# Two heads' value products in alternate column halves, score and turn in one step, and a new placing of the gate pieces in a two-layer hybrid trunk

## The chip, the cores and the metric

The kernel runs on one core of a Trainium2 chip. The metric is the device time of one execution in microseconds, median of the runs shown. Everything is computed in one launch: two layers, 512 latent and 128 context tokens (640 columns together), width 1024.

## The reference

Each layer has a mixer with four branches, a gated merge, an output projection and an MLP. What matters here is the two attention branches and the merge:

```python
# branch A: latent attention, 4 heads, value width 64
s = einsum('bqhd,bkhd->bhqk', q, k) * scale
p = softmax(s);  o_a = einsum('bhqk,bkhd->bqhd', p, v)
# branch D: differential attention, 4 heads, two score maps per head, value width 64
p = softmax(s1) - lam * softmax(s2);  o_d = einsum('bhqk,bkhd->bqhd', p, v)
o_d = rmsnorm(o_d, da_norm_w) * (1 - lam_init)
# merge: four branches, eight blocks of 128 output columns each
proj  = einsum('blnc,ncd->blnd', [o_a, o_b, o_c, o_d], w_branch)
gates = sigmoid(h @ w_gate)
mix   = sum_n(gates * proj) @ w_out
x     = x + gt_a * mix
```

Latent queries see all 640 keys, context queries only the 128 context keys. All data is fp32; the dense products with `h` and with the merged sum are made of three fp32r products each (high x high, high x low, low x high).

## The kernel before

**Layout.** Activations lie transposed, features on partitions, 640 tokens in columns. There is no scheduler: each engine's program is written out by hand in loops, and semaphores (`signal`, with `nth(l, n)` for the n-th event of layer l) order the engines. Every queue is in order.

**Units.** A head times a block of 128 queries is a unit; 4 heads x 5 blocks make U = 20 units of latent attention (called the MLA half) and 20 of differential attention (the differential half), 40 in all, in the order of `FU`. The fifth block of each head holds the context queries and has one key tile instead of five; such a unit is called short here. A unit v has these steps: `score` (TensorE, one map in the MLA half, two in the other, into PSUM banks `ps_aux`), `row_max` (VectorE), `exp` (ScalarE), `combine` (VectorE: normalise, and in the differential half subtract the second map; line 2466 is its last instruction there), `turn` (TensorE: five transposes into `ps_dense` columns 0 to 640), `turned` (ScalarE: copy to SBUF, line 1794), `values` (TensorE, line 1333: per key tile one product with 64 stationary columns, the head's values, so that a head of even number fills PSUM partitions 0 to 63 and one of odd number 64 to 127), and `take_values` (VectorE, line 2474).

**Gates.** The merge has 32 gates i = 0 to 31, eight per branch in the order B, C, A, D. A gate is cut into five parts c = 0 to 4. Parts 0 to 3 are two of eight k tiles each of the dense product (`split_tile`, line 736, twelve matmuls a part); part 3 also has `rows_of` (line 759, sixteen records with 32 stationary columns) for one block of the modulation. ScalarE then takes the hyperbolic tangent (line 1771), VectorE copies the rows (`keep_rows`, line 2551). Part 4 needs both: `turn_rows` (line 766) and `projected` (line 1261), the branch's projection, which VectorE multiplies with the gate (`proj_used`, lines 2423 and 2426) and adds (`gate_sum`, line 2434). Part 0 of the next gate waits for `proj_used`.

**Weights.** SyncE loads a gate's weights in two DMAs; ScalarE makes `w_high` (line 1566) of gate i + 1 at part 2 of gate i, GpSimd then makes `w_low` (line 657, one instruction of 1024 elements).

**The stream.** In `attention`, 24 of the 32 gates (`N_FLOW`) run between the units' steps. TensorE's order is fixed: for each v, `turn(v-1)`, one part, `score(v)`, one part, `values(v-1)`, one part; 120 parts between 3 x 40 steps. ScalarE, VectorE and GpSimd have the same order for what belongs to it. One buffer each holds the MLA half's probabilities (`prob`) and their transposes (`prob_t`).

**merge and out_proj.** The other 8 gates, all of branch D, run in `merge` in one piece each, with `diff_sum` (line 1444) behind the first one's dense product: it sums the squares for the norm of branch D, ScalarE makes the root (`diff_root`, lines 1826 and 1827), VectorE multiplies (line 2497, `br_done`), and only then the rows and the projection of that gate follow. `out_proj` multiplies the merged sum with `w_out`, eight blocks, into the same PSUM banks `ps_dense`.

## Time and profile before

| | us |
|---|---|
| median of 3 runs | 3095.86 |
| lowest, highest | 3094.11, 3096.72 |
| profiled execution, its own time | 3100.46 |
| span of its trace | 3098.9 |
| TensorE matmuls busy | 2907.4 (94%) |
| VectorE, ScalarE, GpSimd busy | 1058.2, 809.3, 656.1 |
| mean granted TensorE clock | 0.976 |

The profile splits the span by engine, by stretch and by line. TensorE is busy nearly throughout, so its own work and its waits make the time; the other engines' busy times count only where TensorE waits for them. The attention of layer 0 lies at 525 to 915 us of the span and `merge` at 915 to 1014; those of layer 1 at 2041 to 2431 and 2431 to 2530, with the same rows to a few tenths. One fp32 matmul stands as two records in the trace, so the ten records of line 1333 are five products. The interval between the starts of two rows that follow each other on TensorE is the time the first one takes there; the busy time of a row reaches a little into the next, because matmuls are pipelined.

### The profile page before, as it was taken

The page shows a single profiled execution, that of the slowest core. Times are in us where ns is not written, and L with a number is a line of the kernel's source. Part 1 is how long each engine was busy: PE and PEld are TensorE (multiplying, and loading weights), DVE is VectorE, ACT ScalarE, POOL GpSimd, SP SyncE. Part 2 cuts the span into 40 slices and gives each one's busy share as a digit, 9 for nine tenths or more (in the row PEclk, how much of TensorE's full clock was granted, in tenths as well). Part 3 has the DMA queues.
Part 4 walks back from the last instruction along what each step waited for, and adds up shares of the span by engine and source line. Part 5 has one row for each costly group of instructions (what it writes and reads, how often), then busy time and mean ns, then how long its engine had stood idle before and what let it go on. Part 6 is the DMA issues. An engine that isn't in the chain of part 4 may idle for free.

```text
span 3098.9 us, 55916 instructions
## 1 busy us (share of the span) xinstructions
PE 2907.4 (94%) x23136; PEld 2426.2 (78%) x23136; DVE 1058.2 (34%) x1984; ACT 809.3 (26%) x1214; POOL 656.1 (21%) x428
## 2 busy tenths in 40 slices
PE   6999999999999899999989998999999998999997
PEld 3558855777778799999956697567777788999997
DVE  1546613224543331111244574132355324111113
ACT  2131023222331241221221411232233214221222
POOL 0102102111212323333301110021121122333332
PEclk9999999999999999999999999999999999999999
DMA  7110011222124222323230100112221232222222
GB/s 301 38 43 10 3 43 36 77 77 77 62 77 135 96 75 90 96 83 96 83 135 25 42 4 10 52 48 77 77 77 63 100 112 90 83 96 89 89 91 81
DMA packets 56671, 235.54 MB, mean 76 GB/s; under 512 B 6624, under 2 KB 6784, under 8 KB 55136
## 3 DMA queue, kind: packets, MB, share of 16 engines
q1 hardware_dynamic: 53568, 206.67, 20.2%
q0 software_dynamic: 2848, 25.13, 2.2%
q8 instruction: 202, 3.31, 0.4%
q14 instruction: 53, 0.43, 0.0%
HBM read 222.96 MB, written 8.81 MB: 75 GB/s over the span
## 4 chain that ended last, share of the span: by engine, by line
PE 89%; DVE 4%; issue 3%; ACT 2%; DMA 1%; POOL 0%; SPq 0%; DVEq 0%; POOLq 0%; ACTq 0%
PE ps_dense L736 47%; PE ps_dense L729 13%; PE ps_dense L1261 4%; PE ps_aux L1312 3%; PE ps_dense L1333 2%; PE ps_aux L1058 2%; PE ps_aux L1038 2%; PE ps_aux L1050 2%; PE ps_aux L1261 1%; PE ps_aux L759 1%; DMA w_ring<-in_w_early 1%; PE ps_dense L1324 1%; PE ps_dense L759 1%; PE ps_dense L1107 1%; PE ps_dense L1399 1%
## 5 line engine op out<-in xcount | busy, mean ns | idle before, releaser
L657 POOL TENSOR_TENSOR w_low<-w_ring,w_high 128x1024 fp32r<-128x1024 f32 x208 | 512.6, 2465 | 1089.4 <-ACT w_high L1566 1087.9
L736 PE MATMUL ps_dense<-h_high,w_high 128*128 128x320 f32 x2048 | 491.8, 321 | 55.5 <-DVE h_low L1979 21.8
L736 PE MATMUL ps_dense<-h_high,w_low 128*128 128x320 f32 x2048 | 468.9, 310 | 0.0
L736 PE MATMUL ps_dense<-h_low,w_high 128*128 128x320 f32 x2048 | 468.7, 310 | 0.0
L729 PE MATMUL ps_dense<-h_norm,w_ring 128*128 128x512 f32 (+1 forms) x1536 | 434.7, 444 | 18.7 <-ACT h_norm L1591 10.6
L729 PEld LDWEIGHTS ps_dense<-h_norm,w_ring 128*128 128x128 f32 x1536 | 240.3, 195 | 217.7 <-issue 206.7
L736 PEld LDWEIGHTS ps_dense<-h_high,w_high 128*128 128x128 f32 x2048 | 336.5, 190 | 79.1 <-issue 44.0
L1566 ACT ACTIVATE w_high<-w_ring 128x1024 fp32r<-128x1024 f32 x208 | 218.9, 1053 | 534.2 <-PE ps_dense L736 433.5
L736 PEld LDWEIGHTS ps_dense<-h_low,w_high 128*128 128x128 f32 x2048 | 344.9, 189 | 0.0
L736 PEld LDWEIGHTS ps_dense<-h_high,w_low 128*128 128x128 f32 x2048 | 344.4, 189 | 0.0
L736 PE MATMUL ps_dense<-z_high,w_high 128*128 128x320 f32 x1280 | 296.5, 313 | 13.5 <-POOL w_low L657 13.5
L736 PE MATMUL ps_dense<-z_low,w_high 128*128 128x320 f32 x1280 | 293.8, 311 | 0.0
L736 PE MATMUL ps_dense<-z_high,w_low 128*128 128x320 f32 x1280 | 293.3, 310 | 0.0
L736 PEld LDWEIGHTS ps_dense<-z_high,w_high 128*128 128x128 f32 x1280 | 215.1, 190 | 16.9 <-issue 16.9
L736 PEld LDWEIGHTS ps_dense<-z_low,w_high 128*128 128x128 f32 x1280 | 216.0, 190 | 0.0
L736 PEld LDWEIGHTS ps_dense<-z_high,w_low 128*128 128x128 f32 x1280 | 215.9, 189 | 0.0
L2545 DVE SCALAR_TENSOR_TENSOR x_res<-ps_dense,mod,x_res 128x320 f32<-128x320 f32 (+2 forms) x192 | 72.6, 434 | 343.2 <-PE ps_dense L736 343.2
L2615 DVE CAST z_high<-flow 128x640 fp32r<-128x640 f32 x64 | 31.6, 494 | 390.3 <-ACT flow L1909 390.3
L2446 DVE TENSOR_REDUCE att_s<-ps_aux 128x1 f32<-128x640 f32 (+1 forms) x120 | 86.2, 718 | 193.4 <-PE ps_aux L1312 161.4
L1907 ACT ACTIVATE flow<-ps_dense 128x640 f32<-128x640 f32 x64 | 45.1, 705 | 321.0 <-PE ps_dense L736 321.0
L1261 PE MATMUL ps_dense<-bout,w_ring 128*128 128x128 f32 (+1 forms) x384 | 115.6, 444 | 0.0
L1261 PEld LDWEIGHTS ps_dense<-bout,w_ring 128*128 128x128 f32 x384 | 61.8, 191 | 45.9 <-issue 45.9
(390 smaller groups left out, 3237.7 us busy)
## 6 DMA issues: line engine op xcount, KB each, us to landing
w_ring<-in_w_mlp SPq DMA_DIRECT2D x128, 512.0 KB, 3.7
w_ring<-in_w_gate SPq DMA_DIRECT2D x64, 640.0 KB, 3.9
w_ring<-in_w_late SPq DMA_DIRECT2D x64, 512.0 KB, 4.6
w_ring<-in_w_early SPq DMA_DIRECT2D x48, 512.0 KB, 3.7
w_ring<-in_w_in SPq DMA_DIRECT2D x48, 512.0 KB, 3.6
w_ring<-in_w_out SPq DMA_DIRECT2D x16, 512.0 KB, 3.7
arena<-in_dft POOLq DMA_DIRECT2D x2, 3264.0 KB, 13.1
par<-in_par POOLq DMA_DIRECT2D x3, 1731.0 KB, 7.6
```

The lines of the kernel that those rows point to most:

```text
L657: g.tensor_tensor(w_low[:, n % 2], ring[:, slot, 0:KC, :], w_high[:, n % 2].bitcast(F32), ALU.subtract).then_inc(w_low_in.sem, 1)
L729: last = mm(out[:, a:b], ring[:, j, k, :], rhs[:, k, a:b], start=k == 0, stop=k == KC - 1)
L736: last = mm(psD[:, b, s * 512:s * 512 + HALF], w_[:, par_, k, :], x_[:, k, s * HALF:(s + 1) * HALF], start=k == 0 and x_ is x_high and w_ ...
L759: last = mm(out[32 * (k % 4):32 * (k % 4) + 32], cond_pad[:, k, at:at + 32], ring[:, slot, k, :], start=j == 0 and k < 4, stop=j == of - 1 ...
L1038: last = mm(psA[rows(r), 2 * i, u * 64:(u + 1) * 64], lt[s % 3][rows(r), d, hh, rows(r)], mv, start=True, stop=True)
L1050: last = mm(psA[rows(r), 2 * i, u * 64:(u + 1) * 64], xt[i][rows(r), u], wm[i][rows(r), u], start=True, stop=True)
L1058: last = mm(psA[rows(r), 2 * i + 1, u * 64:(u + 1) * 64], wm[i][rows(r), u], mv, start=True, stop=True)
L1261: last = mm(out[:, a:c], ring[:, 2 * i % RING, KC + k, :], bout[:, BRANCHES[i // KC], k, a:c], start=k == 0, stop=k == 1)
L1312: last = mm(out[:, a:b], qt, k[:, a:b], start=True, stop=True)
L1566: a(w_high[:, n % 2], ring[:, j, 0:KC, :], ACT.Copy).then_inc(w_high_in.sem, 1)
L2446: link(v.tensor_reduce(small_[:, 2 * m, u:u + 1], src, AX.X, ALU.max, negate=True))
L2545: last = v.scalar_tensor_tensor(out=dst[:, p:q], in0=ps, scalar=gate[:, s:s + 1], in1=dst[:, p:q], op0=ALU.mult, op1=ALU.add)
```

## The change

1. **Values in pairs.** `FU` now takes the heads in pairs: 2 x 2 pairs of heads x 5 query blocks, and for each the even and then the odd head. `values(w)` makes the products of both units of a pair, key tile by key tile, even head into partitions 0 to 63 and odd head into 64 to 127 in turn, and waits for the second unit's `turned`. `take_values` copies all 128 partitions at once. `prob` and `prob_t` get a second buffer each, in parameter columns that are no longer needed.
2. **Score and turn in one step.** TensorE runs `score(v+1)` and directly behind it `turn(v)`. ScalarE's order in the differential half is first map's `exp`, `turned(v)`, second map's `exp`.
3. **Placing.** 22 gates are in the stream instead of 24; their 110 parts are placed by `step_places` in the 3 x 20 places ahead of the steps: two or four of a gate's first four parts together, and part 4 by itself. So a step always stands between parts 3 and 4 and between part 4 and the next gate. I call the places of pair w place 0 (ahead of `score(2w+1)` and `turn(2w)`), place 1 (ahead of `score(2w+2)` and `turn(2w+1)`) and place 2 (ahead of `values(w)`).
4. **Merge.** It has 10 gates, the first two of branch A. `diff_sum` stands in the middle of the first one's dense product; `projected` of that gate waits for the root (`do_rs`), and `br_done` is waited for only at the third. The rows go into `ps_dense`, and `keep_rows` follows the tangent.
5. **out_proj** accumulates in `ps_aux`, and its first block no longer waits for `mod_ready`, which now stands ahead of the norm.

```diff
-N_FLOW = 24
+N_FLOW = 22
-            return [(n, hh, tt) for n in (1, 2) for hh in range(H) for tt in range(NT)]
+            return [(n, 2 * pair + r, tt) for n in (1, 2) for pair in range(H // 2) for tt in range(NT) for r in range(2)]
+        def step_places():
+            places = []
+            for i in range(N_FLOW):
+                extra = 3 * U - 2 * N_FLOW
+                places += [5 * i + 2] * ((i + 1) * extra // N_FLOW - i * extra // N_FLOW) + [5 * i + 4, 5 * i + 5]
+            return [0] + places
+        def parts_ahead(n):
+            return range(max(PLACES[n], 2), PLACES[n + 1])
...
-                def values(v):
+                def values(w):
-                    pe.wait_ge(*pt_in.nth(l, v + 1))
+                    pe.wait_ge(*pt_in.nth(l, 2 * w + 2))
                     for k in range(nk):
-                        last = mm(psD[64 * (hh % 2):64 * (hh % 2) + 64, 0, T:T + P],
-                                  vals[:, k if nk > 1 else 5, hh * 64:(hh + 1) * 64], pt[:, k * P:(k + 1) * P],
-                                  start=k == 0, stop=k == nk - 1)
+                        for r in range(2):
+                            pt = prob_t[r] if n_maps == 1 else d_prob_t[:, r]
+                            last = mm(psD[64 * r:64 * r + 64, 0, T:T + P],
+                                      vals[:, k if nk > 1 else 5, (hh + r) * 64:(hh + r + 1) * 64], pt[:, k * P:(k + 1) * P],
+                                      start=k == 0, stop=k == nk - 1)
...
-                for v in range(1, 2 * U):
-                    turn(v - 1)
-                    gate_part(l, 3 * v - 2)
-                    score(v)
-                    gate_part(l, 3 * v - 1)
-                    values(v - 1)
-                    gate_part(l, 3 * v)
+                gate_part(l, 1)
+                for w in range(U):
+                    for v in (2 * w, 2 * w + 1):
+                        for q in parts_ahead(3 * w + v % 2):
+                            gate_part(l, q)
+                        if v + 1 < 2 * U:
+                            score(v + 1)
+                        turn(v)
+                    for q in parts_ahead(3 * w + 2):
+                        gate_part(l, q)
+                    values(w)
...
-                    dense_split(b, b, h_high, h_low, last_of_block=False)
+                    for k in range(KC):
+                        if i == N_FLOW and k == KC // 2:
+                            diff_sum(l)
+                        split_tile(dense_banks(b), b, k, h_high, h_low)
+                    landed(l, B_GATE + 2 * i + 1)
+                    rows_of(tail_rows(b), (2 * i + 1) % RING).then_inc(gate_ps.sem, 1)
+                    pe.wait_ge(*proj_used.nth(l, i))
                     if i == N_FLOW:
-                        diff_sum(l)
+                        pe.wait_ge(*do_rs.nth(l, 1))
+                    if i == N_GATE - KC:
                         pe.wait_ge(*br_done.nth(l, 1))
```

TensorE, differential half, before: the steps of the units between the parts of a gate. Line 1324 is `turn`, 1312 `score`, 736 the dense product, 759 the rows, 1333 `values`, 1261 the projection.

```order
L1324 MATMUL ps_dense<-con,arena 128x128 x5
...
L736 MATMUL ps_dense<-h_high,w_low 128x320 x2
L759 MATMUL ps_dense<-w_ring,cond_pad 32x128 x8
L1333 MATMUL ps_dense<-arena 64x128 x5
...
L766 MATMUL ps_dense<-con,rows_kept 128x2
L1261 MATMUL ps_dense<-bout,w_ring 128x512
L1261 MATMUL ps_dense<-bout,w_ring 128x128
L1261 MATMUL ps_dense<-bout,w_ring 128x512
L1261 MATMUL ps_dense<-bout,w_ring 128x128
...
L1324 MATMUL ps_dense<-con,arena 128x128 x5
```

The same engine and half after the change (line 1376 is `values`, 797 the rows, 1299 the projection, 1350 `score`, 1364 `turn`):

```order
L797 MATMUL ps_dense<-w_ring,cond_pad 32x128 x8
L1376 MATMUL ps_dense<-arena 64x128 x10
...
L804 MATMUL ps_dense<-con,rows_kept 128x2
L1299 MATMUL ps_dense<-bout,w_ring 128x512
L1299 MATMUL ps_dense<-bout,w_ring 128x128
L1299 MATMUL ps_dense<-bout,w_ring 128x512
L1299 MATMUL ps_dense<-bout,w_ring 128x128
...
L1350 MATMUL ps_aux<-arena,q_pad_odd 128x512
...
L1364 MATMUL ps_dense<-con,arena 128x128 x5
```

One values step has the ten products of two heads where each of two steps had five; score and turn are neighbours.

ScalarE, differential half, before: both maps' exponentials (line 1784) stand together, the copy of the turned unit (1794) between units.

```order
L1794 ACTIVATE arena<-ps_dense 128x640
...
L1784 ACTIVATE arena,att_s<-ps_aux,att_s 128x640
...
L1784 ACTIVATE arena,att_s<-ps_aux,att_s 128x640
...
L1566 ACTIVATE w_high<-w_ring 128x1024
```

After (lines 1830, 1840, 1613 for the same three):

```order
L1830 ACTIVATE arena,att_s<-ps_aux,att_s 128x640
...
L1840 ACTIVATE arena<-ps_dense 128x640
...
L1830 ACTIVATE arena,att_s<-ps_aux,att_s 128x640
...
L1613 ACTIVATE w_high<-w_ring 128x1024
```

The copy moved between the two exponentials, and `w_high` still follows the second one directly where a part 2 comes next.

TensorE at the start of `merge`, before and then after: line 1444 becomes 1487.

```order
L736 MATMUL ps_dense<-h_high,w_low 128x320 x2
L1444 MATMUL ps_aux<-arena,con 128x512
L1444 MATMUL ps_aux<-arena,con 128x128
L1444 MATMUL ps_aux<-arena,con 128x512
L1444 MATMUL ps_aux<-arena,con 128x128
L759 MATMUL ps_aux<-w_ring,cond_pad 32x128 x8
```

```order
L1487 MATMUL ps_aux<-arena,con 128x512
L1487 MATMUL ps_aux<-arena,con 128x128
L1487 MATMUL ps_aux<-arena,con 128x512
L1487 MATMUL ps_aux<-arena,con 128x128
L774 MATMUL ps_dense<-h_high,w_high 128x320 x2
L774 MATMUL ps_dense<-h_low,w_high 128x320 x2
```

The sum of squares has moved from behind the dense product into it, so that half of the product follows it.

## Rows read from the trace of the kernel before

**Rows 1.** page, chain that ended last: shares by engine
```profile
PE 89%; DVE 4%; issue 3%; ACT 2%; DMA 1%; POOL 0%; SPq 0%; DVEq 0%; POOLq 0%; ACTq 0%
```

**Rows 2.** stretches: busy us per engine, granted clock, DMA
```profile
525.00:915.00 390.00, 371.55 (x2494) 299.95 (x2493) 154.89 (x362) 114.73 (x213) 82.84 (x74) 0.99 0.20 72
916.62:938.22 21.60, 15.22 (x85) 11.50 (x83) 5.13 (x7) 6.93 (x6) 2.39 (x1) 0.84 0.16 55
948.58:958.78 10.20, 10.20 (x75) 8.85 (x76) 3.26 (x6) 1.76 (x2) 2.95 (x2) 1.00 0.45 149
```

**Rows 3.** TensorE's waits, 525:915: releaser, us in total, times, longest us
```profile
PE ps_dense L736 <- DVE rs L2426: 5.5, 10, 0.6
PE ps_dense L736 <- POOL w_low L657: 3.8, 1, 3.8
PE ps_dense L1324 <- DVE arena L2474: 3.8, 4, 1.0
PE ps_dense L736 <- DVE x_res L2423: 2.7, 5, 0.6
PE ps_dense L766 <- DVE rows_kept L2551: 2.6, 5, 0.8
```

**Rows 4.** TensorE in time order, MLA half: start, us, what [idle before]
```profile
549.23 0.46 PE L736 MATMUL ps_dense<-h_high,w_low 128*128 128x320 f32 x2
549.61 1.31 PE L1333 MATMUL ps_dense<-stage,arena 128*64 128x128 f32 x10
550.85 0.56 PE L736 MATMUL ps_dense<-h_high,w_high 128*128 128x320 f32 x2
...
552.71 0.71 PE L1324 MATMUL ps_dense<-con,bout 128*128 128x128 f32 x5
553.17 0.54 PE L736 MATMUL ps_dense<-h_high,w_high 128*128 128x320 f32 x2
```

**Rows 5.** TensorE in time order, delta-rule scan, alternating halves
```profile
304.79 1.09 PE L1127 MATMUL ps_dense<-arena 128*64 128x128 f32 x16
305.81 1.16 PE L1133 MATMUL ps_dense<-arena,bout 128*128 128x128 f32 x8
```

**Rows 6.** TensorE in time order, the border of two gates
```profile
560.00 2.41 PE L1261 MATMUL ps_dense<-bout,w_ring 128*128 128x512 f32 x8
562.25 0.71 PE L1324 MATMUL ps_dense<-con,bout 128*128 128x128 f32 x5
563.41 0.53 PE L736 MATMUL ps_dense<-h_high,w_high 128*128 128x320 f32 x2 [0.46 <-DVE x_res L2423]
```

**Rows 7.** all engines in time order, two units of the differential half
```profile
818.32 0.89 DVE L2466 SCALAR_TENSOR_TENSOR arena<-arena,att_s 128x640 f32<-128x640 f32 x1
...
822.01 2.32 PE L1312 MATMUL ps_aux<-arena,q_pad_odd 128*128 128x512 f32 x8
...
824.09 0.54 PE L736 MATMUL ps_dense<-h_high,w_high 128*128 128x320 f32 x2
...
826.20 1.04 ACT L1566 ACTIVATE w_high<-w_ring 128x1024 fp32r<-128x1024 f32 x1
...
827.30 3.10 DVE L2466 SCALAR_TENSOR_TENSOR arena<-arena,att_s 128x640 f32<-128x640 f32 x1
827.33 2.40 POOL L657 TENSOR_TENSOR w_low<-w_ring,w_high 128x1024 fp32r<-128x1024 f32 x1 [2.21 <-ACT w_high L1566]
```

**Rows 8.** all engines in time order, first gate of merge
```profile
926.10 1.33 ACT L1826 ACTIVATE arena<-ps_aux,con 128x1280 f32<-128x1280 f32 x1 [2.86 <-PE ps_aux L1444]
...
930.11 1.49 DVE L2497 TENSOR_TENSOR bout<-arena 128x1280 f32<-128x1280 f32 x1 [10.67 <-ACT arena L1827]
931.66 1.08 PE L759 MATMUL ps_aux<-w_ring,cond_pad 128*32 128x128 f32 x16 [5.59 <-DVE bout L2497]
932.67 4.64 PE L1261 MATMUL ps_aux<-bout,w_ring 128*128 128x512 f32 x8
```

**Rows 9.** GpSimd in time order, start of attention
```profile
529.33 9.35 POOL L651 TENSOR_TENSOR h_low<-h_norm,h_high 128x640 fp32r<-128x640 f32 x6
```

204 lines of the change are left out of this document (111 added, 93 removed).

## The prediction

> **What bounds the kernel now.** I read the chain of work that ended last first: 89% of the span is TensorE [rows 1]. So two things make the time: what TensorE has to do, and what it waits for. The stretches come next: in one layer's attention TensorE is busy for 371.6 of 390 us, the 8% that DMA and the third that VectorE and ScalarE need lie beside it, and a gate of `merge` that waits for nothing takes 10.2 us while the first one takes 21.6 at a granted clock of 0.84 [rows 2]. Then the waits of TensorE in the attention: 5.5 + 2.7 us for the gate's product (`proj_used`), 2.6 for the kept rows, 3.8 for the normalised probabilities, together 14.6 us in 24 waits of under 1 us; and 3.8 us once for the first `w_low`, which the change does not touch [rows 3]. The second layer has the same waits.
>
> **The values.** A full unit's product takes 1.24 us from its start to the next part's [rows 4], ten records at 0.124 us, and about 0.09 us of lead-in ahead of it (the pair of records ahead of it began at 549.23, and such pairs follow each other at 0.29), so 1.33 us a unit and 2.66 a pair. The nearest row for alternating halves is line 1127 in the delta-rule scan: the same shape, 128 rows by 64 columns with 128 moving columns, other weights and other moving data in turn, accumulated into one bank; 16 records take 1.02 us from start to start [rows 5], 0.064 each. A pair then has 20 x 0.064 + 0.09 = 1.37 us and saves 1.29. A short pair has 4 x 0.064 + 0.09 = 0.35 instead of 2 x 0.36 and saves 0.37. A layer has 16 full and 4 short pairs: 20.6 + 1.5 = 22.1 us. The bounds: no gain from alternation would leave 20 x 0.124 + 0.09 = 2.57 a pair, a saving of only 0.09 x 16 = 1.4 us a layer; I take the row of the same shape, and no row of a lower price exists for a gain beyond it.
>
> **Waits in the stream.** Here the placing gives and takes. At the border of two gates TensorE ends the projection at 562.25, does a turn (0.46 us, the distance of the last two lines of [rows 4]) and goes on at 563.41, 1.16 us after the projection [rows 6]: that is the time `proj_used` needs when VectorE is free. In the MLA half a score and a turn (1.0 + 0.46) or a pair of values (1.37) cover it, and the unit's own chain (maximum, exponential, normalising) is over some 3 us after its score, ahead of the next turn. I cost these at nothing, and with cover missing at 0.5 us each as now. Only the short units leave gaps.
>
> In the differential half the chain is longer. The score of 822.01 ends at 824.09; the second exponential ends at 826.2, where ScalarE goes on to `w_high`; the last VectorE step of `combine` starts at 827.30 and takes 0.89 us where nothing disturbs it and 3.10 where `w_low` runs beside it on GpSimd [rows 7]. So the probabilities are ready 4.1 us after the score, or 6.3 us. After the change the copy of the turned unit (0.7 us) stands between the exponentials, which puts 0.6 on both: 4.7 and 6.9. A projection takes about 2.5 us with its turned rows, of which 2.25 are [rows 6]; two parts 0 and 1 take 3.5, parts 2 and 3 with their rows 4.2, two scores 2.1. I go through the places of one layer's differential half:
> - Place 2 holds a part 4 for three units with a full chain. VectorE finishes `combine` at 4.7, multiplies the gate by 5.6; TensorE is there at 0.46 + 2.5 + 1.37 = 4.3, and 1.0 earlier with a short pair. Waits of 1.3, 2.2 (the unit before it late too) and 2.3: 5.8 us.
> - Place 1 holds a part 4 three times: turn 0.46 + 2.5 + score 2.1 = 5.1 covers the chain, the product comes 0.2 late behind the turn: 0.6 us.
> - Place 1 holds parts 2 and 3 twice, with `w_low` beside `combine`: 0.46 + 4.2 + 2.1 = 6.8 against 6.9 and a signal: 0.6 us.
> - Place 2 holds parts 2 and 3 twice, likewise: `keep_rows` stands behind `combine`, so the rows come at 7.35, TensorE arrives at 6.0 or, behind short steps, at 4.7: 1.3 + 2.6 = 3.9 us.
> - Short units leave about 0.65, 0.65, 0.9 and 1.2 us in both halves: 3.4 us.
>
> Together 14.3 us against 14.6 now. So I expect the waits to move rather than to go: the half-microsecond waits at the borders become fewer and longer ones in the differential half. My uncertainty is 10 us less to 8 us more a layer.
>
> On what holds VectorE, the trace shows 3.10 us beside 0.89 [rows 7]. The GPSIMD Engine Reference of the Trainium skill (Specifications) says that GpSimd's SBUF interfaces are shared with VectorE, with contention for instructions with two SBUF inputs or in a two-port mode. The trace agrees for line 2466. By that page `gate_sum`, which has two SBUF inputs as well, could be held too; this speaks against the change, since its tighter order puts more VectorE work behind such a hold, and it is the mechanism of the last rival below.
>
> At the start of the attention one more piece is exposed: the four first parts now come with nothing but value tiles between, while GpSimd makes the last six blocks of `h_low` in 9.35 us from 529.33 on, 1.56 each [rows 9]. The sixth to eighth are there at 537.2 and 538.8, TensorE wants them at 536.7 and 538.1: 1.2 us a layer lost.
>
> **Merge.** The first gate takes 21.6 us. An undisturbed gate takes 10.2 [rows 2], the sum of squares 2.1, and the next gate waits 0.8 for the product as before: 13.1. The rest is the 5.6 us wait for branch D and then half speed (granted clock 0.84 over the stretch): the rows take 1.08 and the projection 4.64 us [rows 8] against 2.4 in [rows 6]. In the new order the sum ends 5.6 us after the gate's start. The root takes 4.0 us from there (926.10 to 930.11 [rows 8]), so `do_rs` comes at 9.7; TensorE ends dense product, sum and rows at 9.8. The root is hidden by half a gate with about nothing to spare, and costs at most its 4 us if the rest of the gate were gone. Branch D itself is wanted 20 us later. New is a wait ahead of the first gate, since the last `take_values` now stands behind the projection's product on VectorE: 1.35 us after the projection, less 0.4 for a short pair, 0.95 us. 13.1 + 0.95 = 14.05 against 21.6: 7.6 us a layer saved. Bounds: 4 with the root exposed, 8.5. Moving two gates from the stream to `merge` costs nothing by itself, both take 10.2 us there.
>
> **out_proj.** It begins when `w_low` of its first block is there, which GpSimd makes behind the last merged block's DMA as before; other banks and a wait placed later than `mod_ready` change nothing. SyncE's DMAs keep their triggers. Nothing, at worst 0.5 us.
>
> **Sum.** A layer: 22.1 + 0.3 + 7.6 - 1.2 = 28.8 us saved, two layers 57.6. The profiled execution had 3100.46 (span 3098.9) and would have 3042.9; the median of the runs is 4.6 us lower, 3095.86, and goes to **3038.3**.
>
> **Rivals.**
> - *The placing works as its form suggests*: VectorE's chain is shorter than I counted, and 10 of the 14.6 us go in each layer. For it: the MLA half already shows no long wait. Against: the 4.7 us chain in the other half. 3038 - 20 = 3018.
> - *The queues bind more*: each of the differential half's late `combine`s also makes the next maximum late, and waits add up to 8 us more a layer, half of it from `w_low` beside `combine`. 3038 + 16 = 3054.
> - *The halves do not overlap in this accumulation*, key tile by key tile in one bank: 2.57 us a pair. Against it is line 1127. 3038 + 2 x 20.7 = 3080, still faster.
> - *Slower*: `w_low` takes VectorE at nearly every gate, now that it always starts right behind an exponential. One hold costs 2.2 us; TensorE would have to pay 29 us a layer more than in my sum, that is more than 1.3 us at each of 22 gates. At the full 2.2 at each it is 48 us a layer: 3038 + 97 = 3135. Cover of 4 to 7 us at most places speaks against it.
> - *It does nothing it says*: values overlap hidden by an equal wait behind them, since turns and copies, not values, set the pace; the time then stays within 0.2%, some 3092.
>
> **How the numbers follow.** 0.60 for the forecast (its own range 3028 to 3048), 0.16 for more binding, 0.13 for less, 0.05 for no overlap, 0.03 for nothing gained, 0.03 for slower. Eight in ten: 3019 to 3062; it leaves out a tail of the less binding case, the halves that do not overlap, and the last two. About 0.2% (6 us) is what a measurement of this kernel can tell from no change: faster 0.94, the same 0.03, slower 0.03.
>
> **What would show it.** The records of the values line at 0.064 us each, some 43 us busy in the whole trace for the 672 of them; a first gate of `merge` of 14 us without a wait for branch D and at full clock; waits of TensorE in the attention of 10 to 20 us, mostly of 1 to 2.5 us, on `proj_used` and the kept rows, after the middle of the attention. Wrong it would be if the values' records stay at 0.12, if the waits in the MLA half grow, or if the gain in `merge` reappears as a wait ahead of `out_proj`.

## The result, and the profile after

| | before | after |
|---|---|---|
| median of the runs | 3096.29 us (3094.11 to 3097.83) | 3020.61 us (3019.37 to 3021.66) |
| profiled execution, span | 3098.9 us | 3018.2 us |

The ratio is 0.9759 (95% interval 0.9746 to 0.9771): 75.7 us less, where the prediction had 57.6 less. The page of the changed kernel begins its chain of work that ended last so (shares of the span by engine; the answer to [rows 1]):

```profile
PE 87%; issue 4%; DVE 3%; ACT 3%; POOL 1%; DMA 1%; SPq 0%; POOLq 0%; DVEq 0%; ACTq 0%
```

TensorE still makes the time. Three stretches follow (length, busy time of TensorE, its weight loads, VectorE, ScalarE and GpSimd, then granted clock, DMA share, GB/s; the answer to [rows 2]): all that lies ahead of attention's first score, attention of layer 0 with the stream, and the first gate of `merge`:

```profile
0.00:517.97 517.97, 469.28 (x4875) 321.36 (x4875) 217.46 (x365) 119.30 (x193) 43.29 (x55) 0.98 0.20 69
517.97:861.77 343.80, 327.69 (x2360) 266.67 (x2359) 154.56 (x338) 106.74 (x210) 80.60 (x72) 0.99 0.22 75
861.77:875.09 13.32, 12.53 (x82) 10.09 (x82) 3.87 (x6) 7.90 (x7) 2.36 (x1) 1.00 0.23 86
```

The kernel before has these two for the first pair:

```profile
0.00:523.53 523.53, 474.41 (x4875) 324.97 (x4875) 217.44 (x365) 119.36 (x193) 43.28 (x55) 0.96 0.20 69
523.53:916.62 393.09, 374.64 (x2508) 301.84 (x2507) 155.08 (x362) 116.79 (x214) 83.80 (x74) 0.99 0.20 72
```

The first 5.6 us of the difference lie ahead of attention, where both kernels have the same 4875 records on TensorE and the granted clock was 0.96 in one execution and 0.98 in the other. They belong to the two executions and not to the change: the profiled one of before was 4.2 us above its median, and the profiled executions of the variants below, whose order is that of the changed kernel up to there, reach the first score at 514.7 to 525.4 us. Attention took 49.3 us less. Two gates of 10.2 us moved out of it, so 28.9 us are a gain.

TensorE's waits in attention of the changed kernel, layer 0 (releaser, us in total, times, longest; the answer to [rows 3]):

```profile
PE ps_dense L774 <- DVE rs L2476: 4.5, 4, 1.9
PE ps_dense L804 <- DVE rows_kept L2601: 4.3, 5, 1.7
PE ps_dense L774 <- POOL w_low L679: 3.8, 1, 3.8
PE ps_dense L1364 <- DVE arena L2517: 1.1, 1, 1.1
PE ps_dense L774 <- POOL h_low L673: 0.7, 2, 0.4
PE ps_dense L774 <- DVE x_res L2473: 0.7, 1, 0.7
```

Without the `w_low` wait, which stayed, and `h_low`, that is 10.6 us in 11 waits where before had 14.6 in 24. TensorE in time order at one pair of heads, MLA half (the answer to [rows 4]):

```profile
544.23 0.32 PE L1376 MATMUL ps_dense<-stage,arena 128*64 128x128 f32 x1
544.23 0.32 PE L1376 MATMUL ps_dense<-par,arena 128*64 128x128 f32 x1
...
545.47 0.56 PE L774 MATMUL ps_dense<-h_high,w_high 128*128 128x320 f32 x2
```

Both heads' records start together. The pair takes 1.24 us to the next part, what one head took before. And `merge` (the answer to [rows 8]), with the start of `out_proj`:

```profile
861.77 0.53 PE L774 MATMUL ps_dense<-h_high,w_high 128*128 128x320 f32 x2 [1.03 <-DVE arena L2524]
...
973.79 0.90 PE L774 MATMUL ps_aux<-z_high,w_high 128*128 128x320 f32 x2 [6.77 <-POOL w_low L679]
```

The first gate takes 13.32 us, at full clock and without a wait for branch D; before it took 21.6. From the first gate of `merge` to `out_proj` there are 112.0 us, where before had 99.9 with two gates (20.4) less: 8.3 us saved. The wait ahead of `out_proj` is the 6.77 us that it was.

The ledger of layer 0 is then 28.9 + 8.3 = 37.2 us, where the prediction had 28.8. Layer 1, read by the same marks, gives 28.1 + 8.1. Both together are 73.4 us, near the 75.7 of the medians.

### The profile page after: what moved, and what is told of

The parts are those of the page before. It is cut to its first block, busy times and chain, and to the rows that moved or that the text cites. A ratio compares the mean times of both kernels' runs of the same rounds, so it can differ in the third digit from the quotient of the medians.

```text
span 3018.2 us, 55846 instructions
## 1 busy us (share of the span) xinstructions
PE 2843.2 (94%) x23136; PEld 2384.0 (79%) x23136; DVE 1061.4 (35%) x1944; ACT 798.2 (26%) x1214; POOL 659.2 (22%) x428
## 4 chain that ended last, share of the span: by engine, by line
PE 87%; issue 4%; DVE 3%; ACT 3%; POOL 1%; DMA 1%; SPq 0%; POOLq 0%; DVEq 0%; ACTq 0%
PE ps_dense L774 43%; PE ps_dense L767 14%; PE ps_aux L774 4%; PE ps_aux L1350 3%; PE ps_dense L1299 3%; PE ps_aux L1096 2%; PE ps_aux L1076 2%; PE ps_aux L1088 2%; PE ps_aux L1299 1%; PE ps_dense L1376 1%; PE ps_dense L1364 1%; DMA w_ring<-in_w_early 1%; PE ps_dense L797 1%; PE ps_aux L797 1%; POOL w_low L679 1%
## 5 line engine op out<-in xcount | busy, mean ns | idle before, releaser
L774 PE MATMUL ps_dense<-h_high,w_high 128*128 128x320 f32 x2048 | 482.6, 317 | 52.8 <-DVE h_low L2029 22.2
L774 PE MATMUL ps_dense<-z_high,w_high 128*128 128x320 f32 x1024 | 235.6, 311 | 0.0
L774 PE MATMUL ps_dense<-z_low,w_high 128*128 128x320 f32 x1024 | 233.3, 309 | 0.0
L774 PE MATMUL ps_dense<-z_high,w_low 128*128 128x320 f32 x1024 | 233.2, 309 | 0.0
L774 PEld LDWEIGHTS ps_dense<-z_high,w_high 128*128 128x128 f32 x1024 | 170.4, 188 | 3.2 <-issue 3.2
L774 PEld LDWEIGHTS ps_dense<-z_high,w_low 128*128 128x128 f32 x1024 | 171.2, 188 | 0.0
L774 PEld LDWEIGHTS ps_dense<-z_low,w_high 128*128 128x128 f32 x1024 | 171.1, 188 | 0.0
L1299 PE MATMUL ps_dense<-bout,w_ring 128*128 128x512 f32 (+1 forms) x352 | 109.3, 455 | 0.0
L2601 DVE COPY rows_kept<-ps_dense 128x128 f32<-128x128 f32 x64 | 18.5, 290 | 254.7 <-ACT stage L1818 147.4
```

The lines of the kernel that those rows point to most:

```text
L774: last = mm(out[:, s, 0:HALF], w_[:, par_, k, :], x_[:, k, s * HALF:(s + 1) * HALF], start=k == 0 and x_ is x_high and w_ is w_high, stop= ...
L1299: last = mm(out[:, a:c], ring[:, 2 * i % RING, KC + k, :], bout[:, BRANCHES[i // KC], k, a:c], start=k == 0, stop=k == 1)
```

## The experiments

The theory after this reading: TensorE's column halves run side by side; the placing of parts by gates, not evenly, keeps VectorE's products off the path; the sum of squares amid the first gate hides the root and keeps the clock; and fewer borders between plain fp32 steps and rounded products save TensorE's own time. The last point does not stand, as the split runs below show. What still waits is VectorE's last step of `combine`, held by GpSimd. Each run changes one thing in the changed kernel (3020.6 us) unless it says otherwise, and the ratios are to the kernel before. That kernel had medians of 3095.7 to 3098.9 us beside the runs of this section and 3096.3 beside the changed one, so a difference of two medians is good to some 3 us; where a difference is small, the same marks in the traces are compared as well.

### Values of one head after the other

```
-                    for k in range(nk):
-                        for r in range(2):
+                    for r in range(2):
+                        for k in range(nk):
```

> The changed kernel (3020.6 us), but in the values step all key tiles of the even head come first and then all of the odd head, so that the products of one column half stand behind each other; everything else stays. If the gain of the values is the overlap of the two column halves, ten records of one half take 1.24 us again and a pair 2.57 instead of 1.37: 1.2 us for each of 32 full pairs and about 0.2 for 8 short ones, 40 us in all, 3060 us, and the records of the values line are busy for some 85 us instead of 45. Rival: the gain comes from fewer steps and fewer waits, the order inside the step being indifferent: 3021 us.

Measured 3035.01 us (3031.98 to 3042.71), ratio 0.9801 (0.9782 to 0.9821). TensorE in time order, a pair in this kernel:

```profile
547.54 0.98 PE L1376 MATMUL ps_dense<-stage,arena 128*64 128x128 f32 x7
548.25 0.32 PE L1376 MATMUL ps_dense<-par,arena 128*64 128x128 f32 x1
...
548.63 0.93 PE L1376 MATMUL ps_dense<-par,arena 128*64 128x128 f32 x7
549.49 0.56 PE L774 MATMUL ps_dense<-h_high,w_high 128*128 128x320 f32 x2
```

The pair takes 1.95 us, not the 2.57 of no overlap and not the 1.24 of alternation. The second head starts (548.25) while the last three of the first head's ten records are still to run, so the halves overlap even where the program has one after the other, by three records. Alternating is worth 0.71 us a pair, 11.4 us a layer for 16 full pairs, and the stream grew by 7.6 us a layer: beside it the waits shrank by 2.2 us, and a stretch of 3.4 us at half clock that the changed kernel has behind a wait (774.20, below) is not there, which is another 1.7. The expected 3060 was too high, since it had no overlap at the seam; the rival, no effect, is out. Of the 1.33 us that a pair gained (2 x 1.33 before, lead-in included, and 1.24 + 0.09 after), 0.71 is the alternation and 0.62 that one step takes both heads, with one lead-in and an overlap at the seam. The Trainium skill, TensorEngine Tiling (Array Packing), Key Properties, says that tiles work independently and in parallel; this trace agrees, 1.24 us for two heads as for one.

### Parts spread evenly

```
-            places = []
-            for i in range(N_FLOW):
-                extra = 3 * U - 2 * N_FLOW
-                places += [5 * i + 2] * ((i + 1) * extra // N_FLOW - i * extra // N_FLOW) + [5 * i + 4, 5 * i + 5]
-            return [0] + places
+            return [5 * N_FLOW * n // (3 * U) for n in range(3 * U + 1)]
```

`gate_sum` then follows each part's number on VectorE.

> The changed kernel with the 110 gate parts spread evenly over the 60 places, without regard to where a gate ends, so that at many borders no attention step parts the tanh, the kept rows and the product from the part that needs them. At such a border TensorE waits 1.16 us for the product and about as long for the rows. Theory: of 22 gates some half have an open border on one side or the other, so some 12 to 18 us a layer are lost, 3045 to 3056 us. Rival: the places are of little weight, since the differential half's waits (10.6 us a layer in the changed kernel) come from VectorE's queue wherever the parts stand: 3025 us.

Measured 3077.86 us (3075.86 to 3082.37), ratio 0.9935 (0.9918 to 0.9951). Three quarters of the gain went. TensorE's waits in this kernel's stream of layer 0, 521.7:893.5:

```profile
PE ps_dense L800 <- DVE rows_kept L2599: 14.2, 11, 2.2
PE ps_dense L770 <- DVE rs L2472: 12.0, 7, 2.6
PE ps_dense L770 <- DVE x_res L2469: 4.3, 5, 1.0
```

30.5 us against 9.5 for the same three. The direction was right and the size too small: 3045 to 3056 was 12 to 18 us a layer, and the stream took 371.8 us for 343.8, 28.0 more. These waits are 21 of it. Most of the rest is the clock: the stream has six stretches of 3.4 us at half clock where the changed kernel has two, five of them behind waits of 2.1 to 2.6 us, and four more such stretches cost 6.8 us. With even spreading 10 of the 21 borders of gates lie inside a place, with nothing of attention between one gate's last part and the next one's first, and there TensorE meets VectorE's queue bare. Beside even spreading, the placing by gates is worth more than the values' 43 us; the kernel before had yet another placing, so this is not a share of the 75.7.

### The sum of squares behind the dense product

```
-                        if i == N_FLOW and k == KC // 2:
-                            diff_sum(l)
+                    if i == N_FLOW:
+                        diff_sum(l)
```

> The changed kernel with the sum of squares behind the first merged gate's product instead of in its middle. The root takes 4.0 us from the end of the sum and then has only the rows (0.6 us) beside it: a wait of about 3.4 us a layer, 7 us in all, 3027 us; if the granted clock falls after that wait, as it did after 5.6 us in the kernel before, up to 2.5 us a layer more, 3032 us. Rival: the sum's place is indifferent and the whole gain of the merge came from the gates of branch A: 3021 us.

Measured 3034.56 us (3028.5 to 3040.43), ratio 0.979 (0.9774 to 0.9807). TensorE in time order, and the granted clock of the stretch behind it:

```profile
882.82 3.34 PE L1299 MATMUL ps_aux<-bout,w_ring 128*128 128x512 f32 x8 [3.52 <-ACT arena L1877]
```
```profile
882.82:892.00 9.18, 8.48 (x32) 6.90 (x33) 3.29 (x4) 1.50 (x2) 0.29 (x1) 0.63 0.37 129
```

The root is exposed for 3.52 us, as [rows 8] let one expect (4.0), and behind that wait the granted clock fell: 0.63 of full speed over 9.2 us, part of it at the lower level. From `merge`'s first gate (869.29) to `out_proj` (987.50) there are 118.2 us in this kernel for 112.0, so wait and slow stretch make 6.2 us a layer, 12.4 of the 14.0 measured. The expected 3032 with the clock's fall had 5.9 a layer and was right; the median lies 2.6 us above it, and these runs spread over 12 us. The rival, 3021, is out. Half a gate of cover is what keeps `merge` at full speed.

### Two more gates in the stream

```
-N_FLOW = 22
+N_FLOW = 24
```

> The changed kernel with 24 gates in the stream and 8 in the merge, as before the change; the sum of squares still stands in the middle of the first merged gate's product, but that gate is one of branch D again and waits for the branch. Theory: the two gates of branch A in the merge hide the multiplication that finishes branch D; here the gate's projection waits for it, 1.5 us longer than the root, so about 2 us a layer are lost in the merge, and the stream has ten more parts between its steps, which cover some 1 to 2 us of its waits: 3018 to 3024 us. Rival: the two gates are what removed the 5.6 us wait and the half clock behind it: then 7 us a layer come back, 3035 us.

Measured 3015.11 us (3012.08 to 3016.49), ratio 0.9731 (0.9715 to 0.9747): 5.5 us faster, below the expected 3018 to 3024. By the marks of a layer, the stream with 24 gates takes 359.1 us, 5.1 less than 343.8 and two gates of 10.2: its waits are 3.4 us shorter in all, and it has one stretch at half clock fewer (1.7). `merge` loses 1.6: a wait of 1.6 us for branch D came before its projection (3.2 in both layers), and no clock fell behind it. Moving gates from the stream to `merge` was thus no source of the gain, and it cost some.

### A part between score and turn, on TensorE alone

```
-                        for q in parts_ahead(3 * w + v % 2):
+                        ahead = list(parts_ahead(3 * w + v % 2))
+                        for q in ahead[:-1]:
                             gate_part(l, q)
                         if v + 1 < 2 * U:
                             score(v + 1)
+                        gate_part(l, ahead[-1])
                         turn(v)
```

> The changed kernel (3020.6 us), but on TensorE the last gate part of each of the 40 places ahead of a score stands between the score and the turn, as a part did before the change; the other engines' order is the same. Theory: each more switch between the fp32r product of a gate and an fp32 step costs TensorE about 0.1 us, since its first weight load is not hidden (the two traces: the same kinds of steps but the values take 3 to 4 us less a layer after the change): 40 more switches a layer, 4 us a layer, 3029 us, with the stream's waits moving by 3 us either way. Rival: switches cost nothing and the 3 to 4 us are something else: 3020 us or, with part 4 covered less well, up to 3024.

Measured 3088.65 us (3082.66 to 3094.5), ratio 0.9978 (0.9968 to 0.9987): nearly the whole gain was lost, far outside both expectations (what the expectation says of a weight load that is not hidden, no run shows). New waits of 2.3 us stood at the score, for the exponential. My first reading was ScalarE's order: the turned copy, which waits for the turn, stands ahead of the second exponential. The next two runs test that.

### The turned copy last on ScalarE, and with it the split again

```
                         two = v + 1 < 2 * U and FU[v + 1][0] == 2
-                        if two:
-                            exp(v + 1, 0)
+                        for m in range(2 if two else v + 1 < 2 * U):
+                            exp(v + 1, m)
                         turned(v)
-                        if v + 1 < 2 * U:
-                            exp(v + 1, 1 if two else 0)
```

> ScalarE alone is reordered: behind a turn it makes both exps of the next step first and the turned copy last. TensorE has parts of a gate between, and in the run of the changed kernel neither a score nor the value products waited for ScalarE. Theory: the order on ScalarE costs nothing as long as both lie inside that cover: 3018 to 3023 us, the changed kernel's 3020.6, with the waits before TensorE's dense products as they were (10.6 us in the stream of layer 0). Rival: the turned copy comes later by two exps, about 1.2 us, and the value products or the next turn wait for it at some of 32 steps of a layer: over 3030 us. This kernel is also the base for the next one.

Measured 3009.38 us (3008.44 to 3013.32), ratio 0.9727 (0.9715 to 0.974): 11 us faster, which neither side expected. VectorE's last step of `combine` in 519:915 (count, busy us, mean ns, idle before), in the changed kernel and in this one:

```profile
L2517 DVE SCALAR_TENSOR_TENSOR arena<-arena,att_s 128x640 f32<-128x640 f32 (+1 forms) x20 | 33.1, 1653 | 0.7
```
```profile
L2515 DVE SCALAR_TENSOR_TENSOR arena<-arena,att_s 128x640 f32<-128x640 f32 (+1 forms) x20 | 15.6, 778 | 0.7
```

ScalarE, VectorE and GpSimd in time order, at the same unit of the changed kernel and of this one:

```profile
768.19 0.80 ACT L1830 ACTIVATE arena<-ps_aux,att_s 128x640 f32<-128x640 f32 x1
...
768.98 1.05 ACT L1613 ACTIVATE w_high<-w_ring 128x1024 fp32r<-128x1024 f32 x1
...
770.08 3.06 DVE L2517 SCALAR_TENSOR_TENSOR arena<-arena,att_s 128x640 f32<-128x640 f32 x1
770.11 2.35 POOL L679 TENSOR_TENSOR w_low<-w_ring,w_high 128x1024 fp32r<-128x1024 f32 x1 [8.68 <-ACT w_high L1613]
```
```profile
770.72 0.27 ACT L1840 ACTIVATE arena<-ps_dense 128x128 f32<-128x128 f32 x1
...
770.88 1.06 ACT L1613 ACTIVATE w_high<-w_ring 128x1024 fp32r<-128x1024 f32 x1
...
771.82 0.88 DVE L2515 SCALAR_TENSOR_TENSOR arena<-arena,att_s 128x640 f32<-128x640 f32 x1
772.02 2.90 POOL L679 TENSOR_TENSOR w_low<-w_ring,w_high 128x1024 fp32r<-128x1024 f32 x1 [8.86 <-ACT w_high L1613]
```

In the first kernel VectorE started 0.03 us ahead and was held until GpSimd had ended; in the second it started 0.20 us ahead, ran in 0.88 us, and GpSimd took half a microsecond longer. What moved is `w_low`, not `combine`. In both kernels `combine`'s last step starts 1.88 to 1.89 us after the second exponential did (768.19, and 769.94 in the second kernel). `w_high` starts 0.79 us after it where it follows the exponential directly; with the copy last, the copy (of a short unit here, 0.27 us) stands between the two, and `w_high` starts 0.94 us after it here and 1.37 where the copy is a full one (0.7 us). `w_low` comes later by as much, so in this kernel none of the 32 full units of both layers is held, where the changed kernel has 16 held and the kernel before 8. The waits at `rs`, `x_res`, kept rows and turn fall from 10.6 to 6.7 us, and the 1.72 us wait of the changed kernel, which had a stretch at half clock behind it (next window), shrinks to 0.78 with none: 3.9 and 1.7 us, near the 5.5 a layer.

```profile
774.20:777.60 3.40, 3.40 (x9) 1.85 (x8) 0.00 (x0) 0.00 (x0) 0.00 (x0) 0.50 0.00 0
```

The 0.6 us that my prediction put on the exponentials for the copy were 0.3 in most units (second exponential 1.37 us after the first, 1.08 with the copy last or in the kernel before). The true price of the copy's place is that it no longer stands between the exponential and `w_high`. The Trainium skill, Trainium Architecture — The Big Picture (What this means for kernel authors), says that the port pair shared by VectorE and GpSimd is an exclusive lock and no split of bandwidth; the trace agrees with that for this instruction, 3.06 us beside 2.35.

> The kernel with the turned copy last, and on TensorE the last part of each place stands between the score and the turn again, as in the kernel before. The earlier run with this split on TensorE alone was confounded by a score that waited for exp behind a turned copy; with exp ahead of the copy that wait should be gone. What is left is 31 more switches from a step in plain fp32 to the gate's rounded products and back, in each layer. Theory (a switch costs about 0.05 to 0.06 us each way, read from the own time of the gate's records that fell by 3.3 to 4 us a layer): 7 to 9 us above the kernel with the copy last alone, near 3028 us. Rival (switches are free, the fall of own time was the clock or chance): within 3 us of the kernel with the copy last alone.

Measured 3077.58 us (3072.11 to 3082.77), ratio 0.9947 (0.9934 to 0.996), 68 us above its base. The wait at the score is still there, so ScalarE's order was not its cause. All engines in time order at one such place:

```profile
535.71 0.29 DVE L2601 COPY rows_kept<-ps_dense 128x128 f32<-128x128 f32 x1 [11.57 <-ACT stage L1820]
535.92 0.81 DVE L2496 TENSOR_REDUCE att_s<-ps_aux 128x1 f32<-128x640 f32 x1
...
536.96 0.79 ACT L1832 ACTIVATE par<-ps_aux,att_s 128x640 f32<-128x640 f32 x1 [1.28 <-DVE att_s L2497]
...
537.90 1.84 PE L1350 MATMUL ps_aux<-arena 96*128 96x512 f32 x4 [2.29 <-ACT par L1832]
```

The score of this unit had ended by 532.4. Its maximum (line 2496) stands on VectorE behind `rows_kept` of a part that TensorE now makes after the score, so it ran at 535.92; the exponential followed, and the next score had to wait until the bank was read. The cause is VectorE's queue, which was still in the order of the changed kernel. An engine's order can be changed alone only if what the others have queued still comes in that order.

The pair of runs was made for another question: whether a border between an fp32 step and a gate's rounded products costs TensorE time of its own. Both kernels show the same number of records. The turned copy last, then with the split (first to last line of layer 0's stream):

```profile
520.73:857.97 337.24, 324.92 (x2356) 265.26 (x2355) 138.00 (x338) 107.49 (x209) 80.03 (x72) 0.99 0.22 77
```
```profile
519.03:890.27 371.24, 334.93 (x2356) 267.65 (x2355) 135.56 (x338) 108.83 (x209) 79.31 (x72) 0.98 0.20 70
```

The same 2356 records kept TensorE busy for 10.0 us more, and waits made the other 24 of the 34 us a layer. But the 10.0 us are for the most part no border's. They have three parts.
- The clock: the split kernel has four stretches of 3.4 us at half clock in this stream (from 525.0, 538.6, 559.1 and 733.2), the kernel with the copy last has one. Three more cost 5.1 us.
- The waits themselves: a record with nothing behind it counts as busy for its whole 0.27 us, while one that is followed at once hands over after 0.03 to 0.11. With 24 more waits that is 3.9 us by the records' starts.
- What is left, about 1 us, is all that 25 more separate pieces of dense product (64 for 39) can have cost.

The rows of one place show the same. TensorE with the copy last, and with the split:

```profile
570.45 1.25 PE L1350 MATMUL ps_aux<-arena 96*128 96x512 f32 x4
571.54 0.71 PE L1364 MATMUL ps_dense<-con,par 128*128 128x128 f32 x5
```
```profile
570.89 1.24 PE L1350 MATMUL ps_aux<-arena 96*128 96x512 f32 x4
571.88 0.54 PE L774 MATMUL ps_dense<-h_high,w_high 128*128 128x320 f32 x2
572.26 0.46 PE L774 MATMUL ps_dense<-h_low,w_high 128*128 128x320 f32 x2
```

A score takes 1.09 us when a turn follows. When a dense product follows it takes 0.99, and the first dense pair takes 0.38 where each later one takes 0.29 to 0.30: 1.37 against 1.38 for the same records. So the border beside a score or a turn is free, as the rival had it, though the time was not within the rival's 3 us either. It is otherwise beside a step with 64 stationary columns. In the kernel before the dense pair ahead of the values takes 0.38 [rows 4], and the first one behind them 0.40 (550.85 to 551.25), with no shorter record beside it: about 0.1 us on either side.

### VectorE: the gate's product ahead of `combine`

In the odd units, what VectorE does for the parts of place 2 (kept rows, the gate's product) is queued ahead of `combine` of the next unit.

```
+                        if v_ % 2:
+                            for q in parts_ahead(3 * w + 2):
+                                gate_part(l, q)
...
-                    for q in parts_ahead(3 * w + 2):
-                        gate_part(l, q)
```

> The changed kernel with one thing moved in VectorE's order: the kept rows and the gate's product of place 2 come ahead of the next unit's normalising instead of behind it. Theory: the long waits in the differential half (1.9, 1.7, 0.7, 0.9, 1.3 and 0.5 us a layer) come from VectorE being inside the normalising, held by GpSimd's low part or not, when the gate's rows or product are due; with the order changed they go, 6 to 7 us a layer, and the normalising has a values step, a place and a score to hide behind: 3007 to 3010 us. Rival: they come from elsewhere, or the later normalising makes the turn wait instead: 3020 us or more.

Measured 3008.31 us (3004.01 to 3011.34), ratio 0.9721 (0.9705 to 0.9737): 12.3 us faster, as expected. Waits in 519:861:

```profile
PE ps_dense L804 <- DVE rows_kept L2602: 2.6, 4, 0.9
PE ps_dense L774 <- DVE rs L2476: 1.1, 2, 0.6
```

The long waits at `rs` (1.9 at most) are gone, and the turn does not wait more than it did (once, 1.1 us). So it was the place in VectorE's queue, and the hold ahead of it, that TensorE waited for.

### GpSimd: the low part as two instructions

```
-                    g.tensor_tensor(w_low[:, n % 2], ring[:, slot, 0:KC, :], ...)
+                    for k in (0, KC // 2):
+                        last = g.tensor_tensor(w_low[:, n % 2, k:k + KC // 2], ...)
```

> The changed kernel with each low part of a weight block on GpSimd made by two instructions of 512 elements instead of one of 1024. Theory: VectorE's two-input step is held until GpSimd's instruction ends; with two it gets in between, so the mean of the last normalising step falls from 1.98 us (8 of 16 held for 3.1) to about 1.4, and the waits of the stream by 1 to 3 us a layer; each more GpSimd instruction costs a few tenths off the path: 3014 to 3019 us. Rival: it is held for as long as GpSimd has work, however it is cut: the mean stays at 2 us, 3020 us.

Measured 3013.15 us (3010.05 to 3016.01), ratio 0.9736 (0.9719 to 0.9752): 7.5 us faster, 1 us beyond the expected 3014 to 3019. The step of `combine` in 519:915, and one held instance in time order with the GpSimd instruction beside it:

```profile
L2519 DVE SCALAR_TENSOR_TENSOR arena<-arena,att_s 128x640 f32<-128x640 f32 (+1 forms) x20 | 24.3, 1214 | 0.7
```
```profile
774.80 2.00 DVE L2519 SCALAR_TENSOR_TENSOR arena<-arena,att_s 128x640 f32<-128x640 f32 x1
...
774.83 1.29 POOL L680 TENSOR_TENSOR w_low<-w_ring,w_high 128x512 fp32r<-128x512 f32 x1 [8.69 <-ACT w_high L1615]
```

The hold is one GpSimd instruction long: 2.00 us beside 1.29, where it was 3.06 beside 2.35. A hold until GpSimd's whole work ends, the rival, would have kept 3.06. The mean of the step fell from 1653 to 1214 ns.

### GpSimd: `out_proj`'s first low part ahead of its last waits

```
-                    if i + 1 < N_GATE:
-                        low_part(l, i + 1, 2 * (i + 1) % RING)
+                    low_part(l, i + 1, 2 * (i + 1) % RING)
...
-                for m in range(N_OUT):
+                for m in range(1, N_OUT):
```

> The changed kernel with one GpSimd instruction moved: the low part of out_proj's first block is made as soon as its high part is there, ahead of the waits for the last merged blocks, instead of behind them. Theory: the 6.8 us a layer that TensorE waits ahead of out_proj, and the half clock behind it (the first 16 matmuls at 0.267 instead of 0.146 us each, some 2.7 us), are this order alone; TensorE then starts at once and waits at the last k tile only for the last merged block, about 1 us after its time: 7 to 9 us a layer, 3003 to 3007 us. It is only possible because the change moved out_proj to other banks and the wait for the modulation behind it. Rival: the last merged block or the DMA holds it anyway: 3018 us.

Measured 3002.66 us (3000.09 to 3007.08), ratio 0.971 (0.9694 to 0.9726): 18.0 us faster, at the edge of the expected 3003 to 3007. GpSimd in the changed kernel made `w_low` at 971.31, behind the DMA of the last merged block, though `w_high` was done at 961.82 (GpSimd and ScalarE of the changed kernel in time order):

```profile
960.76 1.06 ACT L1613 ACTIVATE w_high<-w_ring 128x1024 fp32r<-128x1024 f32 x1 [5.65 <-DMA w_ring<-in_w_out]
```
```profile
970.75 0.54 POOL L742 DMA_DIRECT2D x_res<-x_kept  x1 [9.64 <-DVE z_low L2619]
971.31 4.67 POOL L679 TENSOR_TENSOR w_low<-w_ring,w_high 128x1024 fp32r<-128x1024 f32 x2
```

TensorE in this kernel goes from the last gate straight on, without idle time:

```profile
965.80 0.55 PE L773 MATMUL ps_aux<-z_high,w_high 128*128 128x320 f32 x2
```

9.0 us a layer is more than the wait of 6.77 (`merge` to `out_proj` takes 105.1 us for 112.0), since in the changed kernel the clock had also fallen. The windows are of the start of `out_proj`, first in the changed kernel and then in this one:

```profile
973.79:978.00 4.21, 4.21 (x16) 4.21 (x17) 0.00 (x0) 0.00 (x0) 2.19 (x1) 0.50 0.00 0
```
```profile
965.80:970.00 4.20, 4.20 (x32) 4.20 (x31) 3.48 (x9) 1.06 (x1) 0.33 (x1) 1.00 0.64 224
```

Half the records in the same time, at 1.2 GHz instead of 2.4: another 2.1 us lost in this window alone.

### The remedies together

> The three remedies that each held alone, together: the gate's product ahead of the combination on VectorE (3008.3 alone), out_proj's first low part made ahead of its last wait on GpSimd (3002.7 alone), each low part as two instructions (3013.2 alone). The second lies in another stage than the other two, so it should add in full (18.0 us); the first and the third remedy the same waits behind the combination, which stood at 10.6 us a layer, so of the third's 7.5 us only 0 to 4 should be left beside the first's 12.3. Expected 2986 to 2991 us. Rival (the remedies add in full): 2983 or below; rival (the gate's product ahead holds the combination up once parts are quicker): over 2995.

Measured 2989.76 us (2984.18 to 2992.32), ratio 0.966 (0.9648 to 0.9673): within the expected 2986 to 2991. The gain of the low part in halves is gone beside the gate's product ahead (12.3 + 18.0 = 30.3 us of two alone, 30.9 of all three): the first and the third were made for the same waits.

> The same three, and 24 gates of 32 in attention's stream rather than 22, which alone gave 3015.1 (5.5 us less than the changed kernel, with rs waits of 7.5 us and waits of 3.2 us for a copy of branch D ahead of the projections). With the gate's product ahead of the combination the rs waits should fall, so that of more gates in the stream the clear gain stays: 3 to 7 us below the kernel with three, near 2983 us. Rival (denser places bring the VectorE queue back on the path, now that the product stands ahead of the combination): within 2 us of the kernel with three, or above it.

Measured 2988.85 us (2984.8 to 2994.1), ratio 0.9661 (0.9648 to 0.9674). With 24 gates alone `rs` and the kept rows waited 3.7 and 2.7 us in layer 0; here it is 1.3 and 1.3, but with three remedies and 22 gates it already was 1.1 and 2.6. The time is the same as with three within what the runs can tell: the rival held in its number, but not its mechanism, since VectorE's queue is not more on the path. The marks show where the expected 3 to 7 us went. The stream takes 355.2 us for the 336.0 of three and two gates more, 1.2 less; 24 gates alone had won 5.1 there, much of it from waits that the other remedies take too. `merge` again loses the 1.6 us wait for branch D. Both kernels are 3.4% faster than before and 1% faster than the change. The turned copy last was not tried with them.

## Why the prediction was right, and where its sizes were off

The direction and the two sources that the sum rests on (values and `merge`) held. The time, 3020.6, lies in the range of eight in ten, 3019 to 3062, but at its lower edge: it is 18 us under the likeliest value, outside the 3028 to 3048 that the forecast itself had, and where the first rival stood (3018). The sum came out low because two terms were too small. Term by term for layer 0:

- **Values, 22.1 us predicted, 23.0 measured.** TensorE's time from each values record to the next record is 43.0 us before and 21.8 after, 21.2 less; 20 lead-ins of 0.09 us fewer, which the term had too, are 1.8. The row of line 1127 gave 0.064 us a record, the pair ran at 0.062. The run with one head after the other shows that alternation is half of it.
- **Waits, 0.3 us predicted (14.6 to 14.3), 4.0 measured (14.6 to 10.6).** This is the first mis-sized term. That waits become fewer and longer held; that none is long in the MLA half did not, for the longest of all, 1.87 us at `rs`, is there (683.6). By releaser the sum looks near: the gate's product came to 5.2 us (`rs`, `x_res`) and the kept rows to 4.3, where my places had 6.4 and 4.5. By place it was not. Eight of the eleven waits, 7.7 us, begin within 14 us of a short unit's score, for which I had added 3.4 us and part of what I gave place 2; between full units only three waits, 2.9 us, are left. The turn waited 1.1 once, which I had at nothing. I also read the 3.8 us of [rows 3] as the wait for the normalised probabilities, while the row names line 2474, `take_values`, which stood behind the held `combine` in VectorE's queue.
- **Start of attention, 1.2 predicted, 0.7 measured** (0.35 and 0.37).
- **Own time of TensorE outside the values: costed at nothing, 3.6 us measured.** This term was missing from the sum. 393.1 - 343.8 = 49.3 us less in attention; two gates are 20.4, values 23.0, waits net 2.3 (4.0 less 0.7 at the start and 1.0 ahead of `merge`), which leaves 3.6. By the starts of the records, 1.6 us are first dense pairs behind a values step (0.085 us each, 31 before and 12 after), and 1.9 are the last records ahead of waits, of which there are twelve fewer; work at the lower clock takes 1.0 back (before had part of its slow stretch inside a wait), and about 1 us stays open. These parts are estimates from single rows. That score and turn now stand in one step is no part of it: the split run's rows put a border beside them at 0.01 us.
- **Merge, 7.6 us predicted, 8.3 less 1.0 measured.** The first gate took 13.32 us for 13.1; the new wait for `take_values` was 1.03 for 0.95. The root was hidden by half a gate as counted, and moving the sum behind the gate exposes 3.5 us.
- **out_proj: 0 predicted and found**; the wait of 6.77 us is the same in both kernels. I took it as given, and it was the cheapest gain left (18 us).

The sum of the measured terms is 37.2 us in layer 0 for 28.8. The first rival's 3018 was met for less than half of its reason: it named 20 us in waits, and 8 came from there; the others came from TensorE's own time and from the values. The GpSimd holds did become more, as the slower rival said, 16 of 32 full units for 8, but at most places there was cover. `gate_sum` was not held once in the changed kernel; each of its instructions took 0.82 us. Even parts and a TensorE order that VectorE doesn't share show how the slower rivals would have looked: 57 and 68 us. One slip without consequence: DMA's share in attention is 0.20 [rows 2], not 8%.

## What to carry to other kernels

Count the steps with fewer stationary columns than the work around them: each paid about 0.1 us ahead and 0.1 behind here, so doing two of them in one step saves that even when nothing overlaps. Between a score or a turn of 128 columns and the dense product there was nothing to save. When the same records keep an engine busy for longer, look at its clock and at the records ahead of its waits before blaming the order. When one engine's order is changed, write the order of every engine that serves it anew, and look at which instruction of VectorE will start together with one of GpSimd: a tenth of a microsecond decided between 0.9 and 3.1. A wait that the change doesn't touch is worth the same look, for a queue order that puts ready work behind an unready one costs the wait and the clock behind it.

## What the runs showed of the hardware that was not expected

- Matmuls into the two column halves overlap without being issued in alternation: 3 records at the seam of two heads (1.95 us a pair instead of 2.48), and fully when alternated (1.24).
- A step with 64 stationary columns costs TensorE about 0.1 us on either side beside dense products (a pair of 0.38 and one of 0.40 us for 0.29); a step with 128 costs nothing (1.37 us against 1.38).
- VectorE's last instruction of `combine`, with two SBUF inputs, is held to the end of one GpSimd instruction if that starts from 0.09 us before it to 0.03 us after it, and is not held if it starts 0.11 us after or later. No instance in the traces of the fourteen kernels is otherwise.
- A wait of 3.52 us on TensorE was followed by a granted clock of 0.63 over 9.2 us, one of 6.77 us by 0.50 over 4.2 us. Shorter waits went both ways: behind 1.72 us (773.40 in the changed kernel) stood 3.4 us at half clock, behind 1.87 and 1.60 none, and behind six waits of 2.29 us in the split kernel three did.
